# Sums of squares over attention heads: one full-array product each, or four 64x64 products on the quarters of the array

## The chip, the cores and the metric

The kernel runs on one core of a Trainium2 chip. The metric is the device time of one execution in microseconds (us). A core has TensorE (matrix products into the eight banks of PSUM), VectorE, ScalarE and GpSimd, and SyncE, which here issues the DMAs. Engines run on their own and meet through semaphores.

## The reference

Two layers of a hybrid decoder for 256 tokens of width 1024, then a last RMS norm. In each layer three groups of heads of 64 features (6 gated-DeltaNet, 4 retention, 6 mLSTM heads) share an input and an output projection; a mixture of experts (32 experts, two per token) follows. What the change touches are the sums over the 64 features of a head:

```python
def head_rms(x):
    return x * lax.rsqrt(jnp.mean(x * x, axis=-1, keepdims=True) + EPS)

def l2norm(x):
    return x * lax.rsqrt(jnp.sum(x * x, axis=-1, keepdims=True) + EPS)

# gdn_mixer
q = l2norm(to_heads(q, GDN_HEADS))
k = l2norm(to_heads(k, GDN_HEADS))
...
return from_heads(head_rms(o)) * norm_gain * jax.nn.silu(z)
```

`head_rms` also ends the retention and the mLSTM heads. All numbers are float32.

## The kernel before

Activations lie transposed: features on the 128 partitions, 256 tokens along the free axis, so a tile of 128 partitions holds two heads. A sum over the features of a head, wanted on every partition of that head, is a product with the constant `headsum`, a 128x128 matrix with two 64x64 blocks of ones on its diagonal. It comes three times in a layer:

1. In the front of the mixer (L732 to L735) the squares `sqn` of the six query and key tiles are summed two tiles at a time: 512 columns into one bank, ("nrm", 0) to ("nrm", 2) in banks 7, 0 and 1. ScalarE (L1233 to L1239) first loads the table set with Ln and Exp, then per bank takes Ln(sum + eps) into `rn`, gives the bank free, and Exp(-0.5 x) in place. VectorE (L1599 to L1608) multiplies queries and keys with the result.
2. For the three tiles of the delta heads (L942, `head_norm`, L894 to L897; banks 2, 6, 7), ScalarE squares the outputs into `gsq` (L1321), TensorE sums a tile of 256 columns, ScalarE's `out_rr` (L1313 to L1317) takes Ln and Exp tile by tile, and VectorE's `head_result` (L1712, L1714) multiplies with gain and gate.
3. The same for the two tiles of the retention heads (L947, banks 0 and 1, squares `rsq` at L1368), and later for three mLSTM tiles, which the change leaves as they are.

The order of the work is written out by hand. Each engine runs its program in order; a static plan (`psum_plan`) gives each product a bank, and the n-th user of a bank waits (`begin`) until the user before has given it free. Two such pairs matter here: the second half of the projection ("gate", 1) follows the front sums in bank 1, and the mLSTM scores ("ms", 4) and ("ms", 5) follow the retention sums in banks 0 and 1. On ScalarE `link` makes the engine wait for its own last operation before what follows. Behind the front sums stand, on TensorE, the second half of ("gate", 0), ("gate", 1), the value transposes, and projections that alternate with the scores of the three head pairs; on ScalarE the copy of ("gate", 0) (L1179), the exponentials of beta (L1243), the copy of ("gate", 1), and those of the decays (L1247). SyncE issues every load in one queue; a load waits for a count of freed buffers, and the loads of the mLSTM floors wait for the three delta results (`mix_ready`). In the expert stage TensorE and the stream of expert weights run side by side.

A float32 product shows as two records in the trace, each with its own weight load.

Of the kernel before, what the change touches and what calls it, by code (L numbers as in the profile page):

```python
# [27 lines left out]
ACT = mybir.ActivationFunctionType  # L28
# [5 lines left out]
T = 256  # L34
TT = T // P
KD = D // P
HD = 64
GH, RH, MH = 6, 4, 6
GP, RP, MP = GH // 2, RH // 2, MH // 2
# [114 lines left out]
def psum_plan():  # L154

    front = [(("gdn", 0), 4), ("ssq", 5), (("gdn", 1), 7), ("gatesT", 6), ("gates", 0), (("gdn", 2), 1), ("rows", 2), ("cols", 3)]
    front += [(("gdn", 3), 4), (("gdn", 4), 5), (("gate", 0), 6)] + [(("nrm", s), (7, 0, 1)[s]) for s in range(3)]
    front += [(("gate", 1), 1)] + [(("vt", p), (6, 2, 3)[p]) for p in range(GP)] + [(("gate", 2), 4)]
    for p, b in enumerate(((6, 2, 3, 1), (5, 6, 3, 0), (2, 4, 5, 6))):
        front += [(("kq0", 2 * p), b[0]), (("kq0", 2 * p + 1), b[1]), (("kq1", 2 * p), b[2]), (("kq1", 2 * p + 1), b[3])]  # L160
    front += [(("gate", 3), 7), (("A", 0), 1), (("A", 1), 0), (("A", 2), 3), (("gate", 4), 6)]

    inv = []
    for lev in range(1, 7):
        inv += [("W", lev, g) for g in range(2)] + [("X", lev, g) for g in range(2)]
        inv += [("Z", lev, g, j) for g in range(2) for j in range(TT)]
    inv = [(name, (i + 2) % 6) for i, name in enumerate(inv)]
    inv += [(("rqk", 0), 7), (("rqk", 1), 6), (("mv", 0), 7)]
    late = [(("mqk", 0), 2), ("u1", 3), ("t1", 6), (("mqk", 1), 4), ("u2", 5)] + [(("o", p), (3, 1, 0)[p]) for p in range(GP)]
    late += [(("rs", h), (2, 6, 7, 5)[h]) for h in range(RH)] + [(("mqk", 2), 4)] + [(("on", p), (2, 6, 7)[p]) for p in range(GP)]  # L170
    late += [(("rv", 0), 3), (("mv", 2), 4), (("o", 3), 5), (("o", 4), 7), (("ms", 0), 6), (("ms", 1), 2), (("on", 3), 0), (("on", 4), 1)]
    late += [(("ms", 2), 3), (("ms", 3), 4), (("ms", 4), 0), (("ms", 5), 1), (("wo", 2), 2), (("o", 5), 6), (("wo", 3), 3), (("o", 6), 7)]
    late += [(("wo", 0), 0), (("o", 7), 5), (("on", 5), 4), (("wo", 1), 1), (("on", 6), 6), (("on", 7), 7)]
    late += [("logits", 4), ("nsum", 6), ("rank", 5)] + [(("xt", i), i) for i in range(4)]
    return front + inv + late


def trunk(nc, x_in, consts, level_masks, params, w_mix, router_w, e_gate, e_up, e_down, gain_final, row_store, out):
# [6 lines left out]
    with ExitStack() as ctx:  # L185
# [3 lines left out]
        def sem(name, each_layer=0):  # L189

            made = ctx.enter_context(nc.semaphore(name))
            per_layer[made.num] = each_layer
            return made
# [82 lines left out]
        def c(name):  # L276
            if name in LATE:
                return late[:, LATE.index(name) * P:(LATE.index(name) + 1) * P]
            return kept[:, KEPT.index(name), :] if name in KEPT else cst[:, CONST.index(name), :]
# [100 lines left out]
        u_ready = sem("u_ready", 2)  # L380
        t1_ready = sem("t1_ready", 1)
        o_sq_ready = sem("o_sq_ready", MIX)
        o_sq_in = sem("o_sq_in", MP)
        o_rr_ready = sem("o_rr_ready", MIX)
        rraw_ready = sem("rraw_ready", 2)
# [79 lines left out]
        def upto(l, s, n):  # L465

            return l * per_layer[s.num] + n
# [125 lines left out]
        def _(pe):  # L593
# [5 lines left out]
            def begin(name):  # L599
                b, n = bank_of[name]  # L600
                if n or l:
                    pe.wait_ge(free[b], upto(l, free[b], n))
                return ps[:, b, :]

            def done(ins, name):
                ins.then_inc(full[bank_of[name][0]], 1)
# [20 lines left out]
            def tile_cm(name, ct, ks=range(KD), ready=None):  # L627

                i = SLOT_OF[name]
                if ct == 0 and ks[0] == 0:  # L630
                    begin(name)
                    have_slot(i)
                bank = ps[:, bank_of[name][0], ct * T:(ct + 1) * T]
                for k in ks:
                    if ready:
                        ready(k)
                    mm = pe.matmul(bank, slot_w(i)[:, k, ct * P:(ct + 1) * P], hT3[:, k, :], start=(k == 0), stop=(k == KD - 1))  # L637
                if ct == WIDTH[name] // P - 1 and ks[-1] == KD - 1:
                    done(mm, name)
                    release()  # L640
                    held.append(name)
# [5 lines left out]
            for l in range(LAYERS):  # L647
# [81 lines left out]
                project_cm(("gdn", 4))  # L729
                tile_cm(("gate", 0), 0)  # L730

                for s in range(3):  # L732
                    bank = begin(("nrm", s))
                    pe.wait_ge(sq_ready, upto(l, sq_ready, s + 1))
                    done(pe.matmul(bank[:, :], c("headsum"), sqn[:, 2 * s:2 * s + 2, :], start=True, stop=True), ("nrm", s))  # L735
                tile_cm(("gate", 0), 1)

                def half(a):

                    return slice(64 * a, 64 * a + 64)  # L740

                project_cm(("gate", 1))

# [150 lines left out]
                def head_norm(cidx, src):  # L894
                    bank = begin(("on", cidx))
                    pe.wait_ge(o_sq_ready, upto(l, o_sq_ready, cidx + 1))
                    done(pe.matmul(bank[:, 0:T], c("headsum"), src, start=True, stop=True), ("on", cidx))  # L897

                def r_scores(h):
                    bank = begin(("rs", h))  # L900
                    r_ = half(h % 2)
                    pe.matmul(bank[:, 0:T], rkf[r_, h // 2, 0:P], kqp[r_, h // 2, 0, :], start=True, stop=True)
                    done(pe.matmul(bank[:, T:384], rkf[r_, h // 2, P:T], kqp[r_, h // 2, 0, P:T], start=True, stop=True), ("rs", h))
# [23 lines left out]
                for h in range(RH):  # L927
                    r_scores(h)
                tile_cm(("mqk", 2), 0)
                for p in range(GP):  # L930
                    head_norm(p, gsq[:, p, :])
                tile_cm(("mqk", 2), 1)
                beside(("rv", 0), range(8))
                beside(("mv", 2), range(8))
# [9 lines left out]
                pe.wait_ge(floors_in, upto(l, floors_in, 16 * MH))  # L944
                pe.wait_ge(earg_ready, upto(l, earg_ready, GH + MH))
                pe.sem_inc(mix_freed, 2)
                for p in range(RP):  # L947
                    head_norm(3 + p, rsq[:, p, :])
                for p in (1, 2):
                    pe.wait_ge(mq_ready, upto(l, mq_ready, 4 + p))  # L950
                    m_scores(p)
# [195 lines left out]
        def _(act):  # L1147
# [39 lines left out]
            for l in range(LAYERS):  # L1187
# [44 lines left out]

                act.preload_act_table_set(LN_EXP)  # L1233
                for s in range(3):
                    bank = get(("nrm", s))
                    ins = act.activation(rn[:, 2 * s:2 * s + 2, :], bank[:, :], ACT.Ln, bias=epsc[:, :])
                    link(ins)
                    act.sem_inc(free[bank_of[("nrm", s)][0]], 1)
                    act.activation(rn[:, 2 * s:2 * s + 2, :], rn[:, 2 * s:2 * s + 2, :], ACT.Exp, scale=-0.5).then_inc(rn_ready, 1)  # L1239
                gates(0)  # L1240
                act.wait_ge(betas_in, upto(l, betas_in, 32))
# [82 lines left out]
                    lgam = math.log(1.0 - 2.0 ** (-5.0 - h))  # L1324
                    act.activation(rprob[h], dist[:, :], ACT.Exp, scale=lgam).then_inc(rdec_ready, 1)

                for p in range(GP):
                    out_rr(p, gsq[:, p, :])

                def mlstm_silu(t):  # L1330
                    act.wait_ge(conv_ready, upto(l, conv_ready, 9 + t + 1))
# [34 lines left out]
                for p in range(RP):  # L1366
                    bank = get(("o", 3 + p))
                    act.activation(rsq[:, p, :], bank[:, 0:T], ACT.Square).then_inc(o_sq_ready, 1)  # L1368
                for p in range(RP):
                    out_rr(3 + p, rrr[:, p, :])  # L1370
                m_abs(0)
                m_square(0)
                m_abs(1)
# [635 lines left out]
```

## Time and profile before

| | us |
|---|---|
| median of 3 runs | 805.38 (804.5 to 805.55) |
| profiled execution, its own time | 804.93 |
| its span, first to last instruction | 803.1 |
| TensorE busy | 770.2 (96% of the span) |
| VectorE busy | 310.9 (39%) |
| ScalarE busy | 206.3 (26%) |
| DMA | 256.57 MB, 319 GB/s over the span |

Busy shares are means over stages with different limits. The chain of waits follows the end of the program back through what released each step, so it tells which engine sets the time where. A merged row of the timeline gives the start of its first instruction and the time to the end of the last one. The granted clock is TensorE's, as a share of full speed.

### The profile page before, as it was taken

To read this page: it belongs to the slowest core of one execution; us is meant where nothing else is said; L and a number is where in the kernel's file an instruction comes from. 1 tells how busy PE (TensorE), PEld (TensorE's weight loads), DVE (VectorE), ACT (ScalarE), POOL (GpSimd) and SP (SyncE) were. 2 spreads that over 40 slices of the span, in tenths; PEclk is the share of its full clock that TensorE was granted. 3 is DMA by queue.
4 is the path that set the end of the run, shared out by engine and by line. 5 is a ranking of instruction groups with operands and counts; after the bars stand their busy time and mean duration, and the time that the engine had idled before them with its cause. 6 is when DMAs were issued, how large, how long until landed. Compare 5 with 4: busy or idle time off the path is not lost.

```text
span 803.1 us, 16515 instructions
## 1 busy us (share of the span) xinstructions
PE 770.2 (96%) x6480; PEld 548.8 (68%) x6480; DVE 310.9 (39%) x740; ACT 206.3 (26%) x438; POOL 3.0 (0%) x11
## 2 busy tenths in 40 slices
PE   9999999999999998899999999999999999999976
PEld 7887788878855554455588778888797555555523
DVE  4776343763611111111268754346634111111102
ACT  2353541532400000000124554327212000001003
POOL 0000000000000000000000000000000000000000
PEclk9999999999999999799999999999999999999989
DMA  9983264498599999999998532656887999999995
GB/s 342 417 265 109 78 236 161 160 367 358 211 422 421 419 421 419 421 422 418 419 416 298 171 105 67 224 198 238 352 318 299 421 421 419 421 420 421 420 421 242
DMA packets 44905, 256.57 MB, mean 319 GB/s; under 512 B 5088, under 2 KB 12576, under 8 KB 16032
## 3 DMA queue, kind: packets, MB, share of 16 engines
q1 hardware_dynamic: 44256, 254.77, 80.1%
q8 instruction: 49, 0.80, 0.4%
q10 hardware_dynamic: 576, 0.81, 0.3%
q14 instruction: 24, 0.20, 0.1%
HBM read 252.86 MB, written 1.64 MB: 317 GB/s over the span
## 4 chain that ended last, share of the span: by engine, by line
PE 73%; DMA 10%; DVE 8%; ACT 5%; issue 2%; DVEq 0%; SPq 0%; ACTq 0%; POOL 0%; POOLq 0%
PE ps L1096 14%; PE ps L637 13%; PE ps L1065 8%; PE ps L961 7%; DMA space<-e_up 7%; PE ps L1117 7%; PE ps L1129 4%; DMA late_buf<-e_down 3%; DVE xn L1481 3%; PE ps L1125 3%; PE ps L852 2%; PE ps L821 2%; PE ps L665 2%; PE ps L807 1%; PE ps L885 1%
## 5 line engine op out<-in xcount | busy, mean ns | idle before, releaser
L637 PE MATMUL ps<-hT,ring 128*128 128x256 f32 x800 | 183.6, 382 | 1.0 <-DVE hT L1513 0.9
L637 PEld LDWEIGHTS ps<-hT,ring 128*128 128x128 f32 x800 | 148.4, 190 | 24.8 <-issue 4.7
L1065 PEld LDWEIGHTS ps<-hT,xn 128*128 128x128 f32 x640 | 73.0, 192 | 10.1 <-issue 8.0
L1065 PE MATMUL ps<-hT,xn 128*128 128x128 f32 x640 | 76.8, 278 | 1.9 <-DVE hT L1837 1.9
L1096 PE MATMUL ps<-space,hT 128*32 128x256 f32 x992 | 65.6, 408 | 10.0 <-DMA space<-e_up 6.2
L1096 PEld LDWEIGHTS ps<-space,hT 128*32 128x32 f32 x992 | 31.2, 115 | 39.5 <-DMA space<-e_up 11.8
L961 PE MATMUL ps<-xn,ring 128*128 128x256 f32 x256 | 58.2, 382 | 0.0
L1117 PE MATMUL ps<-ring,space 128*32 128x512 f32 x416 | 50.9, 598 | 6.6 <-ACT space L1422 6.6
L1837 DVE TENSOR_TENSOR hT<-shapes,sel 128x128 f32<-128x128 f32 x40 | 9.9, 289 | 111.8 <-PE ps L1103 111.5
L961 PEld LDWEIGHTS ps<-xn,ring 128*128 128x128 f32 x256 | 48.0, 190 | 7.1 <-issue 0.7
L1854 DVE TENSOR_TENSOR hT<-ps,gffn 128x512 f32<-128x512 f32 x40 | 27.7, 692 | 49.9 <-PE ps L1065 49.9
L1904 DVE COPY hT<-ps 128x512 f32<-128x512 f32 x18 | 12.5, 692 | 88.4 <-PE ps L1117 88.4
L1418 ACT ACTIVATE hT<-ps 128x256 f32<-128x256 f32 x18 | 6.9, 384 | 152.9 <-PE ps L1096 152.9
L1096 PE MATMUL ps<-ring,hT 128*32 128x256 f32 x752 | 44.7, 380 | 0.0
L1422 ACT ACTIVATE space<-ps 128x256 f32<-128x256 f32 x18 | 6.9, 384 | 143.2 <-PE ps L1110 143.2
L1125 PEld LDWEIGHTS ps<-space,hT 128*128 128x128 f32 x144 | 25.1, 189 | 18.8 <-issue 7.5
L1125 PE MATMUL ps<-space,hT 128*128 128x256 f32 x144 | 36.1, 393 | 0.0
L1129 PE MATMUL ps<-hT,space 128*128 128x512 f32 x72 | 35.9, 621 | 0.0
L1096 PEld LDWEIGHTS ps<-ring,hT 128*32 128x32 f32 x752 | 23.4, 110 | 17.6 <-issue 3.2
L1117 PEld LDWEIGHTS ps<-ring,space 128*32 128x32 f32 x416 | 10.9, 109 | 31.7 <-issue 20.2
L1901 DVE TENSOR_TENSOR hT<-hT,ps 128x256 f32<-128x256 f32 x18 | 7.6, 421 | 54.7 <-PE ps L1096 54.7
L1129 PEld LDWEIGHTS ps<-hT,space 128*128 128x128 f32 x72 | 11.4, 188 | 24.7 <-issue 11.9
(290 smaller groups left out, 908.7 us busy)
## 6 DMA issues: line engine op xcount, KB each, us to landing
ring<-e_down SPq DMA_DIRECT2D x46, 1024.0 KB, 26.7
ring<-e_up SPq DMA_DIRECT2D x36, 1024.0 KB, 14.7
ring<-w_mix SPq DMA_DIRECT2D x33, 1024.0 KB, 9.3
space<-e_up SPq DMA_DIRECT2D x26, 1024.0 KB, 25.5
space<-e_gate SPq DMA_DIRECT2D x24, 1024.0 KB, 18.4
more_buf<-e_gate SPq DMA_DIRECT2D x14, 1024.0 KB, 9.9
ring<-e_gate SPq DMA_DIRECT2D x10, 1024.0 KB, 9.5
late_buf<-e_down SPq DMA_DIRECT2D x8, 1024.0 KB, 25.6
```

The source lines that it names most:

```text
L637: mm = pe.matmul(bank, slot_w(i)[:, k, ct * P:(ct + 1) * P], hT3[:, k, :], start=(k == 0), stop=(k == KD - 1))
L665: mm = pe.matmul(bank[:, ct * T:(ct + 1) * T], slot_w(0)[:, k, ct * P:(ct + 1) * P], hU[:, k, :], start=(k == 0 and ct == 0), stop=(k == K ...
L821: mm = pe.matmul(bank[:, j * T:(j + 1) * T], hT3[:, 4 * behind + k, j * P:(j + 1) * P], w[:, k, :], start=(behind == 0 and k == 0), stop=( ...
L852: mm = pe.matmul(z[j][0:rows_, i * HD:(i + 1) * HD], XC[half(j), h, 0:rows_], WC[half(j), h, :], start=True, stop=True)
L961: mm = pe.matmul(ps[:, b, i * T:(i + 1) * T], w[:, i * P:(i + 1) * P], mixT[:, k, :], start=(k == 0 and i == 0), stop=(k == KD - 1 and i = ...
L1065: mm = pe.matmul(ps[:, 4 + 3 * half_, kk * P:(kk + 1) * P], xn3[:, j, k * P:(k + 1) * P], Psel[:, j, :], start=(j == 0), stop=(j == TT - 1))
L1096: mm = pe.matmul(ps[32 * e:32 * e + 32, 5 + m, 0:DE], hq[:, k, 32 * e:32 * e + 32], w[:, c0:c0 + DE], start=(k == 0), stop=(k == KD - 1), ...
L1117: mm = pe.matmul(ps[32 * e:32 * e + 32, 5 + h, :], hmT[:, f, 32 * e:32 * e + 32], w[:, e * 512:(e + 1) * 512], start=(f == 0), stop=(f == ...
L1125: mm = pe.matmul(ps[:, k // 2, k % 2 * T:(k % 2 + 1) * T], ysb[:, h, k % 4 * P:(k % 4 + 1) * P], PwT[:, 0:T], start=False, stop=False, ski ...
L1129: mm = pe.matmul(ps[:, 2 * j + h, :], PwT[:, j * P:(j + 1) * P], ysb[:, h, :], start=False, stop=False, skip_group_check=True)
L1481: link(dve.scalar_tensor_tensor(out=a, in0=s[:, t:t + T], scalar=w(t), in1=a, op0=ALU.mult, op1=ALU.add))
L1854: TTn(hq[:, half * 4:half * 4 + 4, :], ps[:, 4 + 3 * half, :].rearrange("p (k s) -> p k s", k=4), gq[:, half * 4:half * 4 + 4].unsqueeze(2 ...
```

## The change

The sums of two tiles (A and B) are made as four products of a 64x64 matrix of ones with 64 partitions by 256 columns, one on each quarter of the array. Tile A's halves go to their own halves of one bank, tile B's to the opposite halves of a second bank. ScalarE reads B's bank in two halves and writes each to its own place, so that two tiles need three Lns of 256 columns; then one Exp over both. Both banks are given free together, after the third Ln, on a new semaphore `head_logs`. The front uses six banks (7, 2, 0, 3, 1, 4) instead of three. The delta heads' third tile keeps its single product, and so do the mLSTM tiles.

```diff
@@ psum_plan
-    ... [(("nrm", s), (7, 0, 1)[s]) for s in range(3)]
+    ... [(("nrm", s), (7, 2, 0, 3, 1, 4)[s]) for s in range(6)]
@@ TensorE, front
+                def head_sums(names, src):
+
+                    for t in range(2):
+                        bank = begin(names[t])
+                        for a in range(2):
+                            mm = pe.matmul(bank[half(a if t == 0 else 1 - a), 0:T], ones[half(a), 0:HD], src[half(a), t, :],
+                                           start=True, stop=True)
+                        done(mm, names[t])
+
                 for s in range(3):
-                    bank = begin(("nrm", s))
                     pe.wait_ge(sq_ready, upto(l, sq_ready, s + 1))
-                    done(pe.matmul(bank[:, :], c("headsum"), sqn[:, 2 * s:2 * s + 2, :], start=True, stop=True), ("nrm", s))
+                    head_sums([("nrm", 2 * s), ("nrm", 2 * s + 1)], sqn[:, 2 * s:2 * s + 2, :])
@@ TensorE, output norms
+                def two_head_norms(cidx, src):
+                    pe.wait_ge(o_sq_ready, upto(l, o_sq_ready, cidx + 2))
+                    head_sums([("on", cidx), ("on", cidx + 1)], src)
...
-                for p in range(GP):
-                    head_norm(p, gsq[:, p, :])
+                two_head_norms(0, gsq[:, 0:2, :])
+                head_norm(2, gsq[:, 2, :])
...
-                for p in range(RP):
-                    head_norm(3 + p, rsq[:, p, :])
+                two_head_norms(3, rsq[:, 0:2, :])
@@ ScalarE, front
                 for s in range(3):
-                    bank = get(("nrm", s))
-                    ins = act.activation(rn[:, 2 * s:2 * s + 2, :], bank[:, :], ACT.Ln, bias=epsc[:, :])
-                    link(ins)
-                    act.sem_inc(free[bank_of[("nrm", s)][0]], 1)
+                    bank = get(("nrm", 2 * s))
+                    act.activation(rn[:, 2 * s, :], bank[:, 0:T], ACT.Ln, bias=epsc[:, :]).then_inc(head_logs, 1)
+                    bank = get(("nrm", 2 * s + 1))
+                    for a in range(2):
+                        act.activation(rn[64 * a:64 * a + 64, 2 * s + 1, :], bank[64 - 64 * a:128 - 64 * a, 0:T], ACT.Ln,
+                                       bias=epsc[64 - 64 * a:128 - 64 * a, :]).then_inc(head_logs, 1)
+                    act.wait_ge(head_logs, upto(l, head_logs, 3 * s + 3))
+                    act.sem_inc(free[bank_of[("nrm", 2 * s)][0]], 1)
+                    act.sem_inc(free[bank_of[("nrm", 2 * s + 1)][0]], 1)
                     act.activation(rn[:, 2 * s:2 * s + 2, :], rn[:, 2 * s:2 * s + 2, :], ACT.Exp, scale=-0.5).then_inc(rn_ready, 1)
@@ ScalarE, output norms: two_out_rr(cidx, dst, turn) does the same for ("on", cidx) and ("on", cidx + 1)
-                for p in range(GP):
-                    out_rr(p, gsq[:, p, :])
+                two_out_rr(0, gsq[:, 0:2, :], 1)
+                out_rr(2, gsq[:, 2, :])
...
-                for p in range(RP):
-                    out_rr(3 + p, rrr[:, p, :])
+                two_out_rr(3, rrr[:, 0:2, :], 2)
```

## Rows read from the trace of the kernel before

**Rows 1.** The page, part 1: busy time, share of the span and instructions of each engine.

```profile
PE 770.2 (96%) x6480; PEld 548.8 (68%) x6480; DVE 310.9 (39%) x740; ACT 206.3 (26%) x438; POOL 3.0 (0%) x11
```

**Rows 2.** The chain of waits: start, duration in us, engine, what was written, line.

```profile
53.20 3.72 PE ps L637 x16
...
76.85 0.45 PE ps L769 x4
...
447.70 3.72 PE ps L637 x16
```

**Rows 3.** The timeline, 41 to 62 us: start, us, engine, line, operation, idle before.

```profile
46.93 2.74 PE L735 MATMUL ps<-space 128*128 128x512 f32 x6
...
49.50 7.42 PE L637 MATMUL ps<-hT,ring 128*128 128x256 f32 x32
...
49.77 0.69 ACT L1236 ACTIVATE space<-ps,epsc 128x512 f32<-128x512 f32 x1
50.58 0.63 ACT L1239 ACTIVATE space<-space 128x512 f32<-128x512 f32 x1
51.11 0.67 ACT L1236 ACTIVATE space<-ps,epsc 128x512 f32<-128x512 f32 x1
...
53.20 3.32 PEld L637 LDWEIGHTS ps<-hT,ring 128*128 128x128 f32 x16 [0.48 <-ACTq L1238]
...
56.10 0.43 DVE L1608 TENSOR_TENSOR space<-space,late_buf 128x256 f32<-128x256 f32 x1 [0.15 <-DVE space L1590]
...
60.97 1.13 PE L756 MATMUL ps<-space 64*128 64x512 f32 x4
```

**Rows 4.** Busy time by stretch: length, busy us of each engine, clock, DMA share, GB/s.

```profile
205.00:215.00 10.00, 9.01 (x79) 8.74 (x79) 6.90 (x33) 5.50 (x12) 0.00 (x0) 1.00 0.50 186
215.00:300.00 85.00, 83.11 (x951) 50.54 (x954) 17.52 (x48) 8.82 (x19) 0.00 (x0) 1.00 1.01 416
```

**Rows 5.** The timeline, 134 to 156 us.

```profile
139.89 0.65 PE L885 MATMUL ps<-space 128*64 128x256 f32 x4
...
140.59 0.60 PE L885 MATMUL ps<-space 128*64 128x256 f32 x4
...
147.79 0.47 ACT L1315 ACTIVATE late_buf<-ps,epsc 128x256 f32<-128x256 f32 x1 [3.65 <-PE ps L897]
...
150.18 0.42 ACT L1317 ACTIVATE late_buf<-late_buf 128x256 f32<-128x256 f32 x1
...
153.59 0.35 DVE L1479 TENSOR_SCALAR space<-space 128x256 f32<-128x256 f32 x1 [1.13 <-ACTq L1172]
```

**Rows 6.** The timeline, 156 to 186 us.

```profile
165.07 0.66 ACT L1368 ACTIVATE space<-ps 128x256 f32<-128x256 f32 x2 [0.19 <-ACT late_buf L1269]
...
165.60 1.10 PE L897 MATMUL ps<-space 128*128 128x256 f32 x4 [0.75 <-ACT space L1368]
...
168.63 2.86 PE L961 MATMUL ps<-xn,ring 128*128 128x256 f32 x12
...
177.71 0.43 DVE L1740 TENSOR_TENSOR space<-late_buf,space 128x256 f32<-128x256 f32 x1 [1.47 <-ACT space L1347]
```

**Rows 7.** ScalarE's groups by line and shape, 140 to 185 us: busy, mean ns, idle.

```profile
L1315 ACT ACTIVATE late_buf<-ps,epsc 128x256 f32<-128x256 f32 x3 | 1.4, 464 | 3.7 <-PE ps L897 3.7
...
L1368 ACT ACTIVATE space<-ps 128x256 f32<-128x256 f32 x2 | 0.7, 381 | 0.2 <-ACT late_buf L1269 0.2
```

**Rows 8.** ScalarE's timeline, 203 to 214 us.

```profile
211.97 0.30 ACT L1400 ACTIVATE hT<-hT,ss 128x4 f32<-128x4 f32 x1 [0.19 <-ACT xn L1392]
212.18 0.28 ACT L1401 ACTIVATE hT<-hT,ss 128x4 f32<-128x4 f32 x1
```

**Rows 9.** TensorE in three stretches: length, busy us, granted clock, DMA share, GB/s.

```profile
317.20:319.60 2.40, 0.00 (x1) 1.00 1.01 416
320.90:331.00 10.10, 7.44 (x66) 0.50 1.02 425
...
778.30:785.00 6.70, 5.51 (x48) 0.50 1.02 422
```

More of the change, by code:

```diff
@@ L156, in psum_plan @@
     front = [(("gdn", 0), 4), ("ssq", 5), (("gdn", 1), 7), ("gatesT", 6), ("gates", 0), (("gdn", 2), 1), ("rows", 2), ("cols", 3)]
-    front += [(("gdn", 3), 4), (("gdn", 4), 5), (("gate", 0), 6)] + [(("nrm", s), (7, 0, 1)[s]) for s in range(3)]
+    front += [(("gdn", 3), 4), (("gdn", 4), 5), (("gate", 0), 6)] + [(("nrm", s), (7, 2, 0, 3, 1, 4)[s]) for s in range(6)]
     front += [(("gate", 1), 1)] + [(("vt", p), (6, 2, 3)[p]) for p in range(GP)] + [(("gate", 2), 4)]
@@ L382, in trunk @@
         o_sq_ready = sem("o_sq_ready", MIX)
+        head_logs = sem("head_logs", 15)
         o_sq_in = sem("o_sq_in", MP)
@@ L730, in _ @@
                 tile_cm(("gate", 0), 0)
-                for s in range(3):
-                    bank = begin(("nrm", s))
-                    pe.wait_ge(sq_ready, upto(l, sq_ready, s + 1))
-                    done(pe.matmul(bank[:, :], c("headsum"), sqn[:, 2 * s:2 * s + 2, :], start=True, stop=True), ("nrm", s))
-                tile_cm(("gate", 0), 1)
                 def half(a):
                     return slice(64 * a, 64 * a + 64)
+                def head_sums(names, src):
[5 more added lines that the diff above has]
+                        done(mm, names[t])
+                for s in range(3):
+                    pe.wait_ge(sq_ready, upto(l, sq_ready, s + 1))
+                    head_sums([("nrm", 2 * s), ("nrm", 2 * s + 1)], sqn[:, 2 * s:2 * s + 2, :])
+                tile_cm(("gate", 0), 1)
                 project_cm(("gate", 1))
@@ L1325, in _, with two_out_rr @@
                     act.activation(rprob[h], dist[:, :], ACT.Exp, scale=lgam).then_inc(rdec_ready, 1)
-                for p in range(GP):
-                    out_rr(p, gsq[:, p, :])
+                def two_out_rr(cidx, dst, turn):
+                    bank = get(("on", cidx))
+                    act.activation(dst[:, 0, :], bank[:, 0:T], ACT.Ln, scale=1.0 / HD, bias=epsc[:, :]).then_inc(head_logs, 1)
+                    bank = get(("on", cidx + 1))
+                    for a in range(2):
+                        act.activation(dst[64 * a:64 * a + 64, 1, :], bank[64 - 64 * a:128 - 64 * a, 0:T], ACT.Ln, scale=1.0 / HD,
+                                       bias=epsc[64 - 64 * a:128 - 64 * a, :]).then_inc(head_logs, 1)
+                    act.wait_ge(head_logs, upto(l, head_logs, 9 + 3 * turn))
+                    act.sem_inc(free[bank_of[("on", cidx)][0]], 1)
+                    act.sem_inc(free[bank_of[("on", cidx + 1)][0]], 1)
+                    act.activation(dst, dst, ACT.Exp, scale=-0.5).then_inc(o_rr_ready, 2)
+                two_out_rr(0, gsq[:, 0:2, :], 1)
+                out_rr(2, gsq[:, 2, :])
                 def mlstm_silu(t):
```

## The prediction

> **What bounds the kernel now.** I read the page first: TensorE is busy for 96% of the span, ScalarE for 26% [rows 1]. That alone would make any shortened product a gain. The chain of waits says where it is not one. In the front of the mixer (layer 0, 41 to 85 us) the chain runs over ScalarE's table load and its logarithms, and only from 53.20 us over TensorE, which keeps it to 76.85 and beyond [rows 2]. The timeline of the same stretch shows why [rows 3]. The three key/query sums of squares (L735) start at 46.93 and the next product, the second half of ("gate", 0), at 49.50: 2.57 us for three, 0.86 each. ScalarE reads the first of them only at 49.77, when its table load, behind the last convolution's SiLU, is done; the products have waited almost 3 us for their reader. Then come Ln, Exp, Ln, Exp, Ln, a pair every 1.34 us (49.77, 50.58, 51.11). The third Ln, at about 52.45, frees bank 1, which ("gate", 1) waits for: the weight load of L637 stood idle for 0.48 us until 53.20. So the last logarithm sets this stage's end, and L735 doesn't. The chain passes to TensorE at the same point in layer 1, 394.5 us later [rows 2].
>
> Behind the mixer the expert weights flow at 416 GB/s with a DMA share of 1.01, but between 205 and 215 us the share is 0.50 [rows 4]: the stream then waits for buffers that the mixer frees. I therefore count a delay of the mixer in full, not as something the stream hides.
>
> **Part 1, the front sums on TensorE.** Three products of 128x128 by 512 go, twelve of 64x64 by 256 come. Two half-array products of 512 columns took 1.13 us together, where three full ones took 2.74 [rows 3]; on column halves, two of 256 columns (four records) took 0.65 and 0.60 with the pipeline's tail [rows 5], where one full product of 256 holds the array for 0.43 (half of 0.86). A pair costs little more than one. Nothing before runs four quarters at once. From below, a group of four costs one 256-column product, 0.43 us; from above, four in a row, 1.7. I take 0.5, near the half-array rows: L735's 2.57 us become 1.5. This 1.07 us is worth nothing here: it lies ahead of the bank wait, which grows by it. The banks newly taken (2, 3 and 4) were emptied by steps that VectorE and ScalarE run ahead of the last convolutions; no new wait.
>
> The Trainium skill, "TensorEngine Tiling (Array Packing)", section Tiling Modes, says that changing the tiling mode drains TensorE. The first group on column halves took 0.05 more than the later one [rows 5]; by that rule a group costs 0.55 instead of 0.5, and the sum would be 0.1 higher over both layers.
>
> **Part 2, the front logarithms on ScalarE.** Per pair of tiles one Ln of 512 columns becomes three of 256, since each swapped half needs its own. Ln of 256 takes 0.47, Ln of 512 0.69 and 0.67 [rows 3, 5]. What counts is the pitch of Lns that don't depend on each other. Two squares of 256 columns, 0.38 each, take 0.66 together, a pitch of 0.28 with 0.10 of overlap [rows 6, 7]. Does the 0.09 that an Ln with a bias vector takes more vanish in the overlap? Two tiny operations with a vector operand say no: the first takes 0.30 us and the next starts 0.21 after it, an overlap of 0.09 [rows 8]. So the overlap stays at 0.10 and the pitch of an Ln is 0.37. Bounds: 0.21 (0.67 less 0.47, the price of 256 more columns) and 0.47 (no overlap). From an Ln to its Exp behind the semaphore 0.59 passed at 256 columns and 0.80 at 512. So from first Ln to Exp: now 0.80, then 2 x 0.37 + 0.59 = 1.33, +0.53; twice. In the third pair it counts to the last Ln's end: 0.67 before, 2 x 0.37 + 0.47 = 1.21 then, +0.54. Sum **+1.6 us per layer** on the release of bank 1 (bounds 0.6 and 2.2). TensorE's stretch behind it is unbroken chain [rows 2], so it all counts.
>
> Queued behind on ScalarE: the copy of ("gate", 0), the beta exponentials (which waited for a DMA before, and on which only VectorE's key inputs wait) and the decay exponentials, which wait for ("gate", 1) anyway. VectorE's key inputs, ready at 56.10 + 0.43, come at most 1.6 later; their scores run at 60.97 [rows 3]. Cost nothing while that cover of 4 us stands.
>
> **Part 3, norms of the delta heads (on 0 to 2).** From ScalarE's first Ln at 147.79 to the end of the third Exp (150.18 + 0.42) pass 2.81 [rows 5]. After: 1.33 to a 512-column Exp, 0.53 to the next Ln, 0.59 and 0.42: 2.87, +0.06. The first result comes at 147.79 + 1.33 + 0.63 instead of 147.79 + 0.59 + 0.42, so VectorE starts its head results 0.9 late. The 1.13 us it stood idle before the convolution at 153.59 cover that, barely. SP's floor loads wait for these results (mix_ready at three) and go out 0.9 later too; the expert loads queued behind them wait for buffers anyway. TensorE's saving of 0.3 ends in its wait at 165.60.
>
> **Part 4, norms of the retention heads (on 3, 4).** TensorE waits 0.75 us for ScalarE's first square, then runs two products; from 165.60 to the output projection at 168.63 pass 3.03 [rows 6]. After, it waits for both squares (+0.15) and for the 0.06 of part 3, runs a group in 0.5 and reaches the scores at about 166.4, 0.2 earlier. ScalarE frees banks 0 and 1 together after three Lns, at 166.45 + 1.21 = 167.66; the last scores, 0.65 us, follow, and the projection starts at about 168.4: **-0.2 us per layer**, the 0.06 in it. Each 0.01 of pitch moves this by 0.04 (two Lns here, two in part 3): -0.8 and +0.2 at the bounds. VectorE gets its head results 1.1 late; its idle stretches ahead of the divisions, 1.47 at 177.71 for one [rows 6], cover that.
>
> **Sum.** 1.6 - 0.2 = 1.4 per layer, +2.8. The profiled execution took 804.93 (span 803.1 and 1.8 around it), so 807.7; the median of the runs is 0.45 above that execution, and my number is **808.2**. With no overlap it is 2.2 + 0.2 per layer, 810.2; with the squares' pitch 1.06 - 0.55, 806.4; with the lowest 0.6 - 0.8, 805.0.
>
> **Rivals.**
> *The clock falls in the longer wait.* TensorE would finish ("gate", 0) at about 52 and start ("gate", 1) at 55.0: some 2.9 us idle. In the expert stage 2.4 us without a product were followed by a granted clock of 0.50, 1.2 GHz, for 10.1 us, and near the end it stood at 0.50 for another 6.7 [rows 9]; full speed is 2.4 GHz. There it hid behind DMA, here TensorE is the chain. A stretch at half rate costs half its length, 3.4 us for the shorter one; both held further waits, so one without may be half as long, 1.7. Against it: the work around the wait is full-width. Once in two layers: 809.9 to 811.6; twice up to 815. Chance 0.27, time 811.
>
> *Quarters in a row.* The front takes 5.2 instead of 2.57 and outruns ScalarE's delay (+2.6 per layer), the retention pair adds 0.9: +7 in all, 812. The pairs in rows 3 and 5 speak against it: 0.06.
>
> *Not slower.* If independent Lns keep the squares' pitch of 0.28, the front costs 1.06 and the retention pair gives back 0.55 at the projection: 806.4, inside what can be told. It decides at a pitch of 0.31; rows 8 speak against. Chance 0.12. An outright gain needs less than 0.15, under the lower bound, or a clock fall of today gone: 0.03.
>
> *The delay is swallowed* by the weight stream; the share of 0.50 in rows 4 speaks against. 805.5, chance 0.04.
>
> The forecast itself has 0.48. **Range**: 806.0 to 812.0 holds the not-slower case, the forecast with its upper bound, one fall of the clock and serial quarters; two falls and a swallowed delay are left out. A measurement here tells 0.2%, 1.6 us. Faster than 803.8: 0.03. Within: 0.15. Slower than 807.0: 0.82.
>
> **What would show it.** In the profile after: L735's successor in a block of 1.3 to 1.7 us; nine Lns at a pitch near 0.37; ("gate", 1) released by ScalarE some 1.6 us after 53.20; the granted clock there; the projection 0.2 us earlier against the squares; layer 1 at 394.5 + 1.4. Wrong if ("gate", 1) starts no later, or if TensorE then waits elsewhere, at the first scores or the divisions.

## The result and the profile after

| | before | after |
|---|---|---|
| median of 4 runs, us | 805.46 (804.5 to 805.71) | 820.48 (818.31 to 821.57) |
| profiled execution, us | 804.93 | 818.31 |
| its span, us | 803.1 | 816.5 |

The ratio is 1.0189, with a 95% interval of 1.0174 to 1.0204: the change costs 15.0 us, where 2.8 were forecast. The time is above the range.

The page, part 1 and the clock line of part 2 (granted clock in 40 slices, in tenths), of the changed kernel:

```profile
PE 773.7 (95%) x6532; PEld 549.3 (67%) x6532; DVE 310.6 (38%) x740; ACT 212.0 (26%) x450; POOL 2.9 (0%) x11
...
PEclk9999999989999999899999999999999999999989
```

TensorE's busy time went up by 3.5 us against [rows 1], though its products became shorter. The page doesn't say why; busy time is also what a product takes at a lower clock.

The timeline of the front, layer 0, answers to [rows 3]:

```profile
45.86 1.53 PE L742 MATMUL ps<-space,ones 64*64 64x256 f32 x24
...
47.31 1.28 ACT L1245 ACT_TABLE_LOAD   x1
...
48.61 0.47 ACT L1248 ACTIVATE space<-ps,epsc 128x256 f32<-128x256 f32 x1
...
49.11 0.97 ACT L1251 ACTIVATE space<-ps,epsc 64x256 f32<-64x256 f32 x2
50.26 0.63 ACT L1256 ACTIVATE space<-space 128x512 f32<-128x512 f32 x1 [0.19 <-ACT space L1251]
50.80 0.46 ACT L1248 ACTIVATE space<-ps,epsc 128x256 f32<-128x256 f32 x1
...
52.76 0.63 ACT L1256 ACTIVATE space<-space 128x512 f32<-128x512 f32 x1 [0.51 <-ACT space L1251]
...
53.77 0.96 ACT L1251 ACTIVATE space<-ps,epsc 64x256 f32<-64x256 f32 x2
...
54.83 5.41 PE L638 MATMUL ps<-hT,ring 128*128 128x256 f32 x16 [3.79 <-ACTq L1254]
```

The twelve quarter products (24 records) start at 45.86 and the next product at 47.32: 1.46 us for three groups, 0.49 each. ScalarE's part reads otherwise than forecast. The Lns start at 48.61, 49.11 and 0.49 later: none overlaps its neighbour. From the first Ln to the Exp pass 1.65 us, where 0.81 passed before (49.77 to 50.58), and the last Ln ends at 54.73. TensorE stands idle for 3.79 us. Counted from the table load, ("gate", 1) starts at 54.83 - 47.31 = 7.52, against 53.20 - 48.48 = 4.72 before: 2.8 us later in layer 0. In layer 1 the same difference is 2.5 (457.31 - 450.12, against 447.70 - 442.97). The 0.3 between the layers is one idle stretch: the second Exp of layer 0 starts 0.51 us after the Ln before it, every other of these Exps 0.18 or 0.19 after. What ScalarE waited for there isn't shown. And the sixteen records of ("gate", 1) in the last row took 5.41 us where they took 3.72 in [rows 2]. The table load and ("gate", 1) in layer 1:

```profile
450.12 1.28 ACT L1245 ACT_TABLE_LOAD   x1
...
457.31 5.41 PE L638 MATMUL ps<-hT,ring 128*128 128x256 f32 x16 [3.43 <-ACTq L1254]
```

The table loads of the kernel before, in layers 0 and 1:

```profile
48.48 1.28 ACT L1233 ACT_TABLE_LOAD   x1
...
442.97 1.28 ACT L1233 ACT_TABLE_LOAD   x1
```

The timeline at the retention heads, which answers to [rows 6]:

```profile
169.01 0.66 ACT L1397 ACTIVATE space<-ps 128x256 f32<-128x256 f32 x2 [0.19 <-ACT late_buf L1286]
...
169.72 0.66 PE L742 MATMUL ps<-space,ones 64*64 64x256 f32 x8 [1.63 <-ACT space L1397]
...
170.42 0.47 ACT L1346 ACTIVATE space<-ps,epsc 128x256 f32<-128x256 f32 x1 [0.75 <-PE ps L742]
...
170.92 0.96 ACT L1349 ACTIVATE space<-ps,epsc 64x256 f32<-64x256 f32 x2
...
172.07 1.23 PE L922 MATMUL ps<-space 64*128 64x256 f32 x4 [0.82 <-ACTq L1352]
...
173.66 5.22 PE L973 MATMUL ps<-xn,ring 128*128 128x256 f32 x12
```

The two tiles' quarter products wait 1.63 us for both squares, the last scores another 0.82 for the release of banks 0 and 1. The twelve records of the projection after it took 5.22 us; they took 2.86 before.

Who waited for whom on TensorE, both layers: total us, times, longest.

```profile
PE ps L638 <- ACTq L1254: 7.2, 2, 3.8
...
PE ps L742 <- ACT space L1397: 3.2, 2, 1.6
...
PE ps L922 <- ACTq L1352: 1.6, 2, 0.8
```

Five stretches of TensorE (length, busy us, granted clock, DMA share, GB/s): the front's wait, and then every stretch between 40 and 200 and between 430 and 600 us in which the clock was granted at half:

```profile
51.10:54.80 3.70, 0.00 (x0) 1.00 0.88 257
55.60:59.00 3.40, 3.40 (x10) 0.50 0.94 357
171.70:178.40 6.70, 6.33 (x19) 0.50 1.00 385
458.40:461.70 3.30, 3.30 (x10) 0.50 0.87 313
574.50:577.80 3.30, 3.30 (x12) 0.50 1.01 417
```

The clock is 1.00 (2.4 GHz) while TensorE stands idle from 51.1 to 54.8, and 0.50 (1.2 GHz) from 55.6 on, when it works again. It stays there for 3.4 us; behind the retention pair for 6.8; in layer 1 for 3.4 and 3.4. Together 17.1 us at half rate, almost all of it busy, cost half of that, 8.5 us. In the kernel before the same two parts of the trace ran at 1.00 throughout.

The table loads split the difference between the two executions by place. From the load of layer 0 to that of layer 1 pass 402.81 us (450.12 - 47.31) for 394.49 (442.97 - 48.48), 8.3 more; from there to the end of the span 366.4 for 360.1, 6.2 more. The delay at the front, half of the time at half clock and 0.36 us for the retention pair (measured in `e2_out_only` below) make 2.8 + 5.1 + 0.36 = 8.3 in layer 0 and 2.5 + 3.4 + 0.36 = 6.3 in layer 1. So both arrive behind the expert stage in full. Together the two stretches are 14.6 us longer, 1.2 more than the spans' difference of 13.4, because this execution reached its first table load 1.2 us earlier than that of before (47.31, 48.48); that start lies between 47.1 and 48.8 in all fifteen profiles. The fit within 0.1 is partly luck: the same sum misses by up to 1.2 us in other profiles (`e4_filled`, layer 1).

### The profile page after: what moved, and what is told of

The parts are those of the page before. It is cut to its first block, busy times and chain, and to the rows that moved or that the text cites. A ratio compares the mean times of both kernels' runs of the same rounds, so it can differ in the third digit from the quotient of the medians.

```text
span 816.5 us, 16633 instructions
## 1 busy us (share of the span) xinstructions
PE 773.7 (95%) x6532; PEld 549.3 (67%) x6532; DVE 310.6 (38%) x740; ACT 212.0 (26%) x450; POOL 2.9 (0%) x11
## 4 chain that ended last, share of the span: by engine, by line
PE 72%; DMA 10%; DVE 9%; ACT 5%; issue 2%; DVEq 0%; SPq 0%; ACTq 0%; POOL 0%; POOLq 0%
PE ps L638 14%; PE ps L1108 13%; PE ps L1077 7%; PE ps L973 7%; DMA late_buf<-e_down 7%; PE ps L1129 7%; PE ps L1141 4%; DMA ring<-e_down 3%; DVE xn L1509 3%; PE ps L1137 3%; PE ps L861 2%; PE ps L830 2%; PE ps L666 2%; PE ps L816 1%; PE ps L894 1%
## 5 line engine op out<-in xcount | busy, mean ns | idle before, releaser
L638 PE MATMUL ps<-hT,ring 128*128 128x256 f32 x800 | 187.1, 388 | 8.1 <-ACTq L1254 7.2
L638 PEld LDWEIGHTS ps<-hT,ring 128*128 128x128 f32 x800 | 150.7, 193 | 32.6 <-ACTq L1254 8.0
L973 PE MATMUL ps<-xn,ring 128*128 128x256 f32 x256 | 61.4, 396 | 0.0
L973 PEld LDWEIGHTS ps<-xn,ring 128*128 128x128 f32 x256 | 50.3, 199 | 8.2 <-issue 1.1
```

Of the source, the lines that this page charges most:

```text
L973: mm = pe.matmul(ps[:, b, i * T:(i + 1) * T], w[:, i * P:(i + 1) * P], mixT[:, k, :], start=(k == 0 and i == 0), stop=(k == KD - 1 and i = ...
```

## The experiments

The theory after reading this: ScalarE's three Lns make TensorE wait, and the wait then lowers TensorE's clock. The rival: the quarter products themselves lower it, since they use a quarter of the array each. A second question was what keeps the Lns from overlapping. All runs are compared with runs of the kernel before on the same chip.

### One part at a time

`e1_front_only` keeps the front and takes the output norms back:

```diff
-                two_head_norms(0, gsq[:, 0:2, :])
-                head_norm(2, gsq[:, 2, :])
+                for p in range(GP):
+                    head_norm(p, gsq[:, p, :])
...
-                two_out_rr(3, rrr[:, 0:2, :], 2)
+                for p in range(RP):
+                    out_rr(3 + p, rrr[:, p, :])
```

> The changed kernel with the output norms as before, so only the front sums of squares are on quarters. Theory (longer ScalarE chain, then the clock falls in TensorE's longer waits): the front costs 2.5 us of wait and 1.7 us of half rate per layer, so about 814 us (812 to 817), ('gate', 1) starts 2.5 us or more behind its old place, and the granted clock falls once behind the front in each layer and nowhere else in the mixer. Rival (the quarter products themselves lower the clock): also a fall behind the front, but no more than the share of the quarter products there; it is told apart by the next runs. Rival (the loss sits in the output norms): 808 us or less.

Measured: 812.14 us against 805.07, ratio 1.0098 (1.0079 to 1.0117). The waits ahead of ("gate", 1) are as in the changed kernel (7.2 us in two). The profile has one stretch at half clock in the mixer, 3.4 us behind the front of layer 0, and none behind the equal wait of layer 1. The expectation of a fall in each layer was wrong for this execution; the four runs spread from 811.3 to 814.6.

`e2_out_only` does the reverse (front and its bank plan as before).

> The kernel before with only the output norms changed (two pairs on quarters, three Lns and one Exp per pair). Theory: the longer idle stretches around the retention pair (0.9 becomes 1.8, and a new one of 1.0 before the last scores) let the clock fall there, 1.7 to 3.4 us lost per layer, so 809 to 812 us, with the front unchanged and the granted clock at 1.00 through it. If the two parts simply add, this and the front alone make up the 15 us. Rival (only the front matters): 805 to 806 us.

Measured: 808.31 us against 805.07, ratio 1.0045 (1.0026 to 1.0063), just under the 809 expected, but ten runs from 805.44 to 811.46. The mean granted clock over the span was 0.993 to 0.996 in the three runs below 806 and 0.981 to 0.987 in the six above 807. The profiled one, 805.63, is among the three fastest and had the clock at 1.00 through both mixers. It shows what the retention pair costs alone:

```profile
165.11 0.66 ACT L1393 ACTIVATE space<-ps 128x256 f32<-128x256 f32 x2 [0.19 <-ACT late_buf L1282]
...
165.82 0.66 PE L742 MATMUL ps<-space,ones 64*64 64x256 f32 x8 [1.62 <-ACT space L1393]
...
169.03 2.86 PE L974 MATMUL ps<-xn,ring 128*128 128x256 f32 x12
```

From the squares to the projection pass 3.92 us; before it was 168.63 - 165.07 = 3.56 [rows 6]. So the pair loses 0.36 us per layer where I had it gain 0.2, and the rest of this version's 3.2 us comes in some executions and not in others, with a lower mean clock.

### ScalarE alone

`e3_three_logs` leaves TensorE as before and splits each front Ln:

```diff
-                    ins = act.activation(rn[:, 2 * s:2 * s + 2, :], bank[:, :], ACT.Ln, bias=epsc[:, :])
-                    link(ins)
+                    act.activation(rn[:, 2 * s, :], bank[:, 0:T], ACT.Ln, bias=epsc[:, :]).then_inc(head_logs, 1)
+                    for a in range(2):
+                        h_ = slice(64 * a, 64 * a + 64)
+                        act.activation(rn[h_, 2 * s + 1, :], bank[h_, T:2 * T], ACT.Ln, bias=epsc[h_, :]).then_inc(head_logs, 1)
+                    act.wait_ge(head_logs, upto(l, head_logs, 3 * s + 3))
```

> The kernel before, full-array products and one bank per pair of tiles, but each front Ln of 512 columns split into one of 128x256 and two of 64x256 in place. Theory: ScalarE's chain alone makes the wait: the Lns follow each other at 0.49 us without overlap, the release of bank 1 comes 2.5 us later, 810.5 us if the clock holds and up to 814 if it falls in the wait of about 3 us. Rival (quarter products lower the clock): the clock stays at 1.00 and the time is 810 to 811. Rival (moving halves across partitions is what makes the Lns slow): the Lns overlap here, pitch 0.37 or less, and the time is 808 or less.

Measured: 809.38 us against 805.07, ratio 1.0056 (1.0039 to 1.0073), four runs within 0.6 us. ScalarE's timeline in this kernel:

```profile
50.05 0.47 ACT L1237 ACTIVATE space<-ps,epsc 128x256 f32<-128x256 f32 x1
50.42 0.95 ACT L1240 ACTIVATE space<-ps,epsc 64x256 f32<-64x256 f32 x2
51.49 0.63 ACT L1243 ACTIVATE space<-space 128x512 f32<-128x512 f32 x1
```

The first half's Ln starts 0.37 after the full one, as I had worked out, but the two halves take 0.95 together: the second doesn't overlap the first. The last front Ln ends 2.2 us per layer later than before (2.5 had been expected, without any overlap), twice that is the whole loss, and no stretch of the mixer is at half clock. TensorE's wait is 2.25 us here. So ScalarE's chain passes to the end in full, as forecast, and moving halves isn't needed to make it slow.

`e7_no_bias` is the front-only version with `bias=epsc[...]` taken off the front's Lns (it leaves epsilon out).

> The front-only version with the front's Lns taken without the bias vector; it leaves epsilon out. If the vector operand is what keeps the Lns from overlapping, each takes 0.38 us at a pitch of 0.28, the last Ln ends 1 us per layer after its old time, and the run takes 807 us. If the change of partition range between neighbours does it, they follow each other at 0.38 to 0.41 without overlap, and the time is 808.5 to 810. In both the wait is shorter than in the front-only version (812 us), and a fall of the clock rarer.

Measured: 812.47 us against 804.83, ratio 1.0085 (1.0059 to 1.0110). ScalarE:

```profile
49.79 0.38 ACT L1249 ACTIVATE space<-ps 128x256 f32<-128x256 f32 x1
50.20 0.78 ACT L1252 ACTIVATE space<-ps 64x256 f32<-64x256 f32 x2
```

An Ln without the bias vector takes 0.38 and the next starts 0.41 after it. The 0.09 of the bias vector goes, the lack of overlap stays. The wait was 2.99 us, and in this execution the clock fell behind the front in both layers, 3.4 us each, which is why it took 811.78 us: less the 3.4 us that they cost it would be at 808.4, just under the 808.5 to 810 expected for the shorter chain alone.

`e8_two_logs` is the front-only version with one Ln over all 128 partitions of the second tile's bank; it leaves that tile's halves swapped in the norms.

> The front-only version with the second tile's bank read by one Ln over all 128 partitions, so two Lns per pair; the halves of that tile are not put back, which changes the computed key and query norms. The quarter products stand. Theory (only the Lns over changing halves are serial): the two Lns overlap at a pitch of 0.37, the bank comes 0.5 to 0.6 us later per layer than before the change, no fall of the clock, 806 to 807 us. Rival (every Ln with a bias vector is serial): pitch 0.48, 807 to 808 us. Rival (quarter products lower the clock): a fall behind the front and over 808 us.

Measured: 806.58 us against 804.83, ratio 1.0016 (1.0007 to 1.0026). ScalarE:

```profile
49.86 0.47 ACT L1249 ACTIVATE space<-ps,epsc 128x256 f32<-128x256 f32 x1
50.23 0.47 ACT L1251 ACTIVATE space<-ps,epsc 128x256 f32<-128x256 f32 x1
50.89 0.63 ACT L1255 ACTIVATE space<-space 128x512 f32<-128x512 f32 x1 [0.19 <-ACT space L1251]
```

Two Lns over the same 128 partitions start 0.37 apart, with the bias vector and the quarter products in place. TensorE's wait is 1.6 us, and the clock stays at 1.00 in both mixers. Its total is a rough measure only: the swapped norms change what the second expert stage works on, and TensorE has 6312 records in all, against 6516 in `e1_front_only`, and 29 us at half clock in that stage, against 12.

What keeps the Lns apart is neither the bias vector (`e7_no_bias`) nor the second bank (`e8_two_logs`). The rows fit the partitions that an Ln reads. Behind an Ln over partitions 0 to 127, a half read from 0 to 63 starts after 0.37 us (`e3_three_logs`), and a half read from 64 to 127 after 0.48 to 0.50 (the changed kernel); both are written to 0 to 63. Between two halves with a bias vector it is 0.48, in place or moved. So Lns overlap where the partitions read begin at the same one, and not where they don't. The range written doesn't tell the first two cases apart. In place nothing is moved, and two halves don't overlap either; whether the move across partitions adds something in the changed kernel isn't shown.

### The clock

`e4_filled` is the changed kernel with products of ones in two idle stretches:

```diff
                 tile_cm(("gate", 0), 1)
+                b5 = [n for n, b in psum_plan() if b == 5]
+                pe.wait_ge(free[5], upto(l, free[5], b5.index(("gdn", 4)) + 1))
+                for _ in range(14):
+                    pe.matmul(ps[:, 5, 0:P], ones[:, :], ones[:, :], start=True, stop=True)
...
                 def two_head_norms(cidx, src):
+                    if cidx == 3:
+                        bank = begin(("on", 3))
+                        for _ in range(6):
+                            pe.matmul(bank[:, T:T + P], ones[:, :], ones[:, :], start=True, stop=True)
```

(`b5` lists the users of bank 5, so that the wait is for its last reader.)

> The changed kernel with products of ones put into two of TensorE's idle stretches in each layer: 14 of 128x128 by 128 columns into the free bank 5 ahead of ('gate', 1), 6 into unused columns of bank 0 ahead of the retention pair. They compute nothing that is read. Theory (the waits lower the clock): the granted clock stays at 1.00 behind both places, the waits for ScalarE stay, and the time is 810 to 813 us. Rival (the quarter products lower it): falls in the same places, 818 to 821 us.

Measured: 812.21 us against 805.07, ratio 1.0096 (1.0079 to 1.0113): 8 us less than the changed kernel, with more work and the same releases by ScalarE. ("gate", 1) starts 7.52 us after the table load, as in the changed kernel, and the filling leaves 0.67 us of the wait of 3.79:

```profile
50.67 3.29 PE L753 MATMUL ps<-ones 128*128 128x128 f32 x28
54.63 3.72 PE L638 MATMUL ps<-hT,ring 128*128 128x256 f32 x16 [0.67 <-ACTq L1262]
```

Both mixers in windows of TensorE (length, busy us, granted clock):

```profile
40.00:200.00 160.00, 157.77 (x1118) 1.00 0.60 212
430.00:600.00 170.00, 168.17 (x1167) 1.00 0.57 209
```

`e9_full_long_wait` makes the wait without a quarter product: the kernel before, the front's Ln of 512 columns done three, three and one times.

```diff
-                    ins = act.activation(rn[:, 2 * s:2 * s + 2, :], bank[:, :], ACT.Ln, bias=epsc[:, :])
-                    link(ins)
+                    for _ in range((3, 3, 1)[s]):
+                        ins = act.activation(rn[:, 2 * s:2 * s + 2, :], bank[:, :], ACT.Ln, bias=epsc[:, :])
+                        link(ins)
```

> The kernel before, full-array products, with four of the front's Lns repeated in place, so that ScalarE frees bank 1 about 3.2 us later in each layer and TensorE stands idle for some 3.4 us, as in the changed kernel. Theory (a long enough wait lowers the clock, whatever the products before it): the granted clock falls behind the front in at least one of the two layers, and the time is 813 to 815 us. Rival (it takes the quarter products too): the clock stays at 1.00 through the mixer and the time is 811 to 811.5 us.

Measured: 812.99 us against 804.94, ratio 1.0098 (1.0081 to 1.0114), just under the 813 to 815 expected. TensorE's timeline and a window of it:

```profile
46.46 2.74 PE L735 MATMUL ps<-space 128*128 128x512 f32 x6
49.03 3.62 PE L637 MATMUL ps<-hT,ring 128*128 128x256 f32 x16
55.60 5.41 PE L637 MATMUL ps<-hT,ring 128*128 128x256 f32 x16 [2.95 <-ACTq L1239]
```

```profile
57.05:60.40 3.35, 3.35 (x10) 0.50 0.79 328
```

After 2.95 us of waiting, with full-array products on both sides, sixteen records again take 5.41 us, at half clock. So at the front the quarter products aren't needed for a fall. Layer 1, with a wait of 2.90, kept its clock in this execution.

At the retention heads the same two questions were asked with the output norms alone. `e10_out_filled` adds the six products of ones to `e2_out_only`; `e11_out_full` replaces its quarter products by two full ones, with three Lns in place and a common release.

> The output-norms-only version with six products of ones ahead of the retention pair, in place of 1.3 us of its 1.6 us of idle time; they compute nothing that is read. Theory (the spread of 805.4 to 811.5 us of the version without them is the clock falling at these waits in some executions): all executions between 805 and 806.5 us, and 1.00 through the mixer. Rival (the quarter products lower the clock, or the spread is something else): the same spread as without them.

Measured: 806.40 us (805.96 to 809.16, ten runs) against 804.94, ratio 1.0024 (1.0014 to 1.0033). The spread upwards is smaller than without the filler but not gone, so the expectation of 805 to 806.5 throughout was missed; the 0.82 us wait before the last scores wasn't filled.

> The output-norms-only version with full-array products: two of 128x128 by 256 columns per pair after the wait for both squares, three Lns in place, both banks freed together. Theory (the waits lower the clock, the quarters don't matter): the same idle stretches of 1.6 and about 0.5 to 0.8 us, the same spread upwards from 805.5, median 806 to 810 us. Rival (the quarter products lower the clock): all executions at 805 to 806 us.

Measured: 806.85 us (805.06 to 807.64, seven runs) against 804.94, ratio 1.0022 (1.0009 to 1.0035). The median lies in the theory's range, the spread is narrower than in `e2_out_only`, and so neither expectation is clearly met: the waits came out shorter than in `e2_out_only` (1.4 and 0.3 against 1.6 and 0.8), so the pair isn't a clean test of the quarters here. `e4_filled` shows that they don't lower the clock by themselves, and `e9_full_long_wait` that a long wait does without them. Whether they, or the half-array scores around them, help a wait of 1.6 us to lower it at the retention heads is untested.

### The wait for bank 1

`e5_bank7` is the front-only version with ("gate", 1) in a bank that the first pair frees; `e6_before_bank7` makes the same edit in the kernel before.

```diff
-    front += [(("gate", 1), 1)] + ...
+    front += [(("gate", 1), 7)] + ...
```

> The front-only version with one number changed in the bank plan: ('gate', 1) goes to bank 7, which the first pair's Lns free, instead of bank 1, which the last pair's free. Theory (the loss at the front is the wait for bank 1): ('gate', 1) starts right behind ('gate', 0), at about 51 us in the layer; TensorE then waits up to 1.5 us for bank 6 at the value transposes and perhaps for VectorE at the first scores, but every one of these waits is short, the clock stays at 1.00 behind the front, and the time falls from 812 to 805 to 808 us. Rival (ScalarE's longer chain reaches the scores by VectorE anyway): 810 us or more.

Measured: 806.72 us against 804.83, ratio 1.0023 (1.0013 to 1.0033): of the front's 7 us 1.9 are left. TensorE:

```profile
48.64 7.17 PE L638 MATMUL ps<-hT,ring 128*128 128x256 f32 x32
57.62 0.84 PE L757 MATMUL ps<-shapes,space 128*128 128x128 f32 x6 [1.81 <-ACTq L1195]
```

("gate", 1) follows ("gate", 0) without a break, in one row of 32 records; the wait has moved to the value transposes (bank 6, which ScalarE copies after its last Exp) and is 1.8 us, and the clock stays at 1.00 in both mixers.

> The kernel before with the same one number changed. Theory: the 0.48 us that TensorE's weight load stood idle ahead of ('gate', 1) goes in both layers, and the value transposes are reached 0.3 to 0.5 us earlier: 804.2 to 804.7 us. Rival (what follows waits for ScalarE or VectorE as before): no change.

Measured: 804.50 us against 804.83, ratio 0.9991 (0.9982 to 0.9999). It is the fastest version tried, by less than 0.1%. TensorE's products of that stretch follow each other without the gap. The saving of the quarter products, 1.1 us per layer in the front, isn't in it.

### Why the parts don't add up

The front costs 7.1 and the output norms 3.2 us alone, 10.3 together, but the change costs 15. Two more runs were made for that.

> The changed kernel unaltered, on the chip of the next run. If the 15 us were a property of the first chip's state, it comes out near 815 us, the sum of its two parts measured apart (7 and 3 us). If the parts reinforce each other, 818 to 822 us again, and the profile shows the clock at 0.50 behind the front and in the retention heads' stretch in the same execution.

Measured: 819.87 us (818.75 to 823.45) against 804.87, ratio 1.0199 (1.0171 to 1.0228). It isn't the chip. In this profile the front's wait of layer 0 was not followed by a fall, the retention pair was in both layers, for 6.8 us each, and the front of layer 1 for 3.4: 17.1 us at half clock again, in other places. In layer 0 the clock fell at 169.65, 0.95 us behind the wait of 1.62 and 1 us before the second wait began.

> Full-array front sums with three Lns per pair (a front wait of 2.3 us, at which the clock held before) together with the changed output norms. If the two parts simply add, 805 + 4.3 + 3.2 = 812.5 us. If the output norms are dearer whenever the front has shifted them, 815 us or more. If the excess of the changed kernel comes only from a front wait long enough for a fall, 810 to 813 us.

Measured: 816.67 us (812.76 to 817.16) against 804.87, ratio 1.0136 (1.0106 to 1.0166), 4 us above the sum of its parts and in the range expected if the output norms are dearer whenever the front has shifted them. TensorE at the front and at the retention heads of layer 0:

```profile
54.82 3.72 PE L638 MATMUL ps<-hT,ring 128*128 128x256 f32 x16 [2.25 <-ACTq L1254]
```

```profile
168.03 0.66 PE L742 MATMUL ps<-space,ones 64*64 64x256 f32 x8 [1.62 <-ACT space L1396]
...
170.37 1.23 PE L923 MATMUL ps<-space 64*128 64x256 f32 x4 [0.82 <-ACTq L1351]
...
171.96 5.00 PE L974 MATMUL ps<-xn,ring 128*128 128x256 f32 x12
```

The front's wait (2.25 us, full products) left the clock alone in layer 0. The retention pair's waits were 1.62 and 0.82 us, as in `e2_out_only`. The clock fell at 169.50, between the two, and the projection took 5.00 us, against 2.86 in that version's profile. Layer 1 had a fall of 3.4 us at either place.

So with the front shifted, the same waits of the output norms seem to meet the clock's fall more often. On top of `e3_three_logs` the output norms cost 7.3 us in the median (3.4 to 7.8 in four runs), alone 3.2 (0.4 to 6.4 in ten). In the three profiles with both parts and unfilled waits the clock fell at the retention pair in both layers. The one profile without the front's part shows it in neither, but that execution is one of its version's fastest, and its slower ones had a lower mean clock; it proves little by itself. The 5 us by which the change exceeds its parts fit more falls. Why the shift matters, that is, what besides the waits decides on a fall, stays open.

## Why the prediction was wrong

**What bounds the kernel.** Right. The front's end is set by ScalarE's last Ln: `e3_three_logs` lengthened nothing else, and its loss is twice the shift of that Ln; the table loads show 8.3 and 6.2 us arriving behind the two expert stages; `e5_bank7` took the wait for bank 1 away and most of the loss with it. The delay passed through the expert stage in full, as I had counted it.

**Part 1.** Right in size and in worth: 1.46 us for three groups where I took 1.5. Pairs on half the array were a good guide to four quarters. The drain that the Trainium skill names, "TensorEngine Tiling (Array Packing)", section Tiling Modes, is at most the 0.06 per group above 0.43, and the trace can't tell a drain from weight loads.

**Part 2, the first step that failed: "the overlap stays at 0.10 and the pitch of an Ln is 0.37".** It holds where the next Ln reads from the same first partition on (`e8_two_logs`, `e3_three_logs`: 0.37). In the change no Ln of a group does, and they follow each other at 0.49 with no overlap. It was my upper bound, 0.47, that came nearest, and the term came out at 2.5 to 2.8 us per layer for 1.6 (bounds 0.6 to 2.2). Of the 0.9 us missing in layer 1, 0.7 is the pitch (six times 0.12). The other 0.14 is that the first two Exps start 0.19 after the Ln before them, where I had 0.12; the profiles don't say why. Layer 0 has the 0.3 of the long idle stretch besides. I looked for what makes a single Ln longer and didn't ask whether the rows that showed overlap had anything in common: they all ran over partitions 0 to 127, and no operation of ScalarE in the trace of before covers 64.

**Part 3.** From the first Ln to the third Exp's end pass 3.18 us (151.26 to 154.44) for 2.81: +0.37, for +0.06, by the same 1.65 us from the first Ln to the Exp. **Part 4.** +0.36 for -0.2 (`e2_out_only`). The three Lns take 1.46 us where I had 1.21, and from the last scores' start to the projection pass 0.86 where I had 0.65; the rest is smaller. The sum without the clock is so about 5.3 at the front and, from the lower end of `e2_out_only` and `e10_out_filled`, 0.4 to 1.0 for the output norms, some 6 us where I had 2.8. `e4_filled`, 7.1 with its filled waits, comes near it.

**The clock, the second step that failed.** The mechanism was among the rivals, at 0.27, with the place in the front and a price per fall from rows 9; the forecast itself put it at nothing. Its size was wrong twice. I priced it at one fall in two layers, and I looked for it behind one wait. The retention pair's waits, 1.63 and 0.82 us, stood in my own sum (the square's +0.15, banks freed together) and I didn't hold them against rows 9. The two profiles of the changed kernel have three and four falls, 17.1 us at half clock, 8.5 us lost. The lower price per fall, 1.7, was right for the short ones, the upper, 3.4, for those of 6.8 us at the retention pair. The range ended at 812, having left out "two falls"; three and four were the case.

**The other rivals.** Quarters in a row: excluded by the 1.46 us. A swallowed delay: excluded by `e3_three_logs`. A pitch of 0.28: excluded.

## What to carry to other kernels

A faster product is worth nothing ahead of a wait for the engine that reads it, and dear if its layout gives that engine more instructions: count the reader's instructions first, at their full length where neighbours start at different partitions. A wait of TensorE costs more than its own length when work that sets the end follows it, for the clock may be halved just then; a bank that is freed earlier (`e5_bank7`), or filling the wait (`e4_filled`), can give back more than the wait's own microseconds. And two parts that are each measured alone don't have to add.

## What the runs showed of the hardware

- ScalarE, Ln of 256 columns from PSUM, with a bias vector: start to start 0.37 us between two over partitions 0 to 127 (`e8_two_logs`) and from such a one to a half read from 0 to 63 (`e3_three_logs`); 0.48 to 0.50 to a half read from 64 to 127, 0.48 between two halves, in place or moved. Without a bias vector each takes 0.38, and the moved halves follow at 0.40 to 0.41 (`e7_no_bias`).
- TensorE's clock at the front: after an idle stretch of 2.6 to 3.8 us the granted clock was 0.50 in 7 of 10 profiled cases (both layers of the change, its repetition, `e1_front_only`, `e7_no_bias` and `e9_full_long_wait`), and 1.00 in 3. After 2.2 to 2.3 us it was 0.50 in 1 of 4 (`e3_three_logs`, `e13_logs_and_out`), after 1.4 to 1.8 (`e5_bank7`, `e8_two_logs`) in none of 4. It fell between the last microsecond of the wait and 1.5 us behind it.
- At the retention heads, with quarter products and half-array scores around the waits of about 1.6 and 0.8 us, it was 0.50 in 6 of 8 (the change, its repetition, `e13_logs_and_out`; none in `e2_out_only`), in one of them before the second wait began. With the first wait filled (`e4_filled`, `e10_out_filled`) it was 1.00 in all 4. A stretch at half clock lasted 3.4 or 6.8 us in the mixer.
- Four 64x64 products of 256 float32 columns on the four quarters took 0.49 us, one product of 128x128 by 256 takes 0.43.
